# Half-block products in the down projections of a four-FFN network

## The chip, the cores and the metric

The kernel runs on one NeuronCore of one Trainium2 chip. A run's time is the device time in microseconds (us) from the first to the last instruction of the core. All arithmetic is in float32.

## The reference, cut to what matters

The network has 256 tokens, kept as the columns of tiles of 128 features x 256 tokens. Around a series of mixers (MLA attention, an LRU scan, cross attention, sparse attention, a complex state space scan) stand four feed-forward blocks, each of width 2816:

```
def swiglu(h, w_gate_up, w_down):
    g, u = jnp.split(h @ w_gate_up, 2, axis=-1)
    return (jax.nn.silu(g) * u) @ w_down
```

The last two are the same with a short causal convolution on the 5632 up columns. Each is added to the residual stream x, after which comes the next RMS norm. What is changed is `... @ w_down`: a product of a 1024 x 2816 matrix (transposed weights) with 2816 x 256 activations, four times.

## The kernel before, in words

Each engine has its own instruction list, written out by hand and tied to the others by counting semaphores. There is no planner. All weights come as one stream of 128 x 1024 slots (512 KB) through a ring of four SBUF buffers; SyncE issues the load of slot s as soon as slot s-4 is counted in `slot_used`. The loads of a second weight matrix (`ada_in`, 96 loads of 512 KB) stand between those of the stream, and VectorE folds each into a running sum (`ada(n)`, L1679).

A down projection (`down0` to `down3`) makes eight output tiles of 128 features x 256 tokens. Each is 22 matmuls (k tiles 0 to 21 of FFN, three slots of weights), 128x128 weights against 256 columns, all at L395, accumulated in one of four PSUM banks `acc`. The profiler counts two instructions for each float32 matmul. VectorE adds each finished tile to X in `residual` (L1537, with a gain L1539), makes the gained copy that the next stage's first matmuls read (`gain_tile`, L1506) and sums the squares (L1509); ScalarE squares. The next stage begins with `lead`: its first tiles are multiplied from the gained, not yet normalised X (L450), the sum of squares goes through the ones matrix in between (L431, L432), VectorE makes the reciprocal root (L1468, L1458 to L1461) and then normalises H (L1519, L1522) for the following tiles.

Beside the down projections VectorE has other work in its list: in `down0` six `ada` and, after the third tile, `lru_parameters` (small operations on 8 columns, L1802 to L1817); in `down1` `drive_powers`, eight parts of which six have six 512-wide products (L1897 to L1902); ahead of `down2` `local_kernels` (L1924 to L1934), which clears and fills the matrices of the state space stage. In the third up stage TensorE waits for VectorE's `output_powers` (L1918) before the products of L880. The up stages have 44 tiles each, two for every step k of VectorE's loop.

Of the kernel before, what the change touches and what calls it, by code (L numbers as in the profile page):

```python
# [13 lines left out]
P = 128  # L14
# [57 lines left out]
ADA_FREE = [max((b + 1 for b in range(a) if ADA_HOME[b] == ADA_HOME[a]), default=0) for a in range(N_ADA)]  # L72

# [77 lines left out]
def build_program(nc, stream, ada_in, ssm_in, cols_in, x_in, mem_in, pos_in, out):  # L151
    with ExitStack() as ctx:
# [20 lines left out]
        mem_rstd = sb("mem_rstd", S)  # L173
# [6 lines left out]
        keep = sb("keep", S)  # L180
        restart = sb("restart", S)
# [38 lines left out]
        slot_used = sem("slot_used")  # L220
        acc_free = sem("acc_free")
# [106 lines left out]

        block = ctx.enter_context(nc.Block())
# [3 lines left out]
        def _(sp):  # L333
# [37 lines left out]
        def _(pe):  # L371
# [84 lines left out]

            def value_rows(name, src, n):
# [42 lines left out]

            def down(name):

                n = COUNT[name][1]
                for k in range(n):
                    bank_free(TILE0[name] + k)
                    b = acc[(TILE0[name] + k) % 4]
                    for c in range(3):
                        w = slot_in(name, 3 * k + c)
                        lo, hi = 8 * c, min(8 * c + 8, KF)
                        if k == 0:  # L510
                            pe.wait_ge(ffn_mid, 2 + 22 * int(name[-1]) + hi)
                        product(b[:, 0:S], w, [at(FFN, i) for i in range(lo, hi)], first=c == 0, last=c == 2)\
                            .then_inc(slot_used, 1)
# [228 lines left out]
            linear("od_xb", H, lead([("od_xb", 0), ("od_xb", 1)], gained_in_y), first=2)  # L742
# [17 lines left out]
            fresh = lead([("dki", 0)] + [("dqi", k) for k in range(3)], gained_in_late, S + 1, second=M)  # L760
# [243 lines left out]
        def _(act):  # L1004
# [14 lines left out]
            def norm(src, tiles, first=0, after=None, func=ACT.Sqrt):  # L1019
# [6 lines left out]
                if after:  # L1026
                    for k in range(tiles):
                        act.wait_ge(after[0], after[1] + k + 1)
                        nc.scalar.activation(at(SQ, k), at(src, k), ACT.Square).then_inc(norm_squares, 1)  # L1029
# [8 lines left out]
            def double_norm():  # L1038
# [4 lines left out]
                for k in range(KD):  # L1043
                    act.wait_ge(acc_free, 4 + TILE0["down1"] + k + 1)
                    nc.scalar.activation(at(M, k), at(X, k), ACT.Square, scale=col("final_norm", k))
                    nc.scalar.activation(at(SQ, k), at(X, k), ACT.Square).then_inc(norm_squares, 1)
                for e in range(2):
                    act.wait_ge(norm_vars, n + 1 + e)
                    nc.scalar.activation(root[:], variance[:], ACT.Sqrt).then_inc(norm_rstd, 1)
# [202 lines left out]
            norm(X, KD, after=updated("down0"))  # L1252
# [60 lines left out]
            nc.scalar.activation(keep[:], acc[TILE0["dwi"] % 4][:, 0:S], ACT.Copy).then_inc(wi_parts, 1)  # L1313
# [31 lines left out]
            norm(X, KD, after=updated("down2"), func=ACT.Abs_reciprocal_sqrt)  # L1345
# [65 lines left out]
            conv_ffn("up3", 1)  # L1411

# [29 lines left out]
        def _(dve):  # L1442
# [86 lines left out]
            def residual(name, slots_per_tile=1, gain=None, adas_with=0, drive=False, next_gain=None, gained_in=None):  # L1529
                begin(name)  # L1530
                for k in range(8):
                    if drive:
                        drive_powers(k // 4, k % 4)
# [8 lines left out]
                    if name != "down3":  # L1542
                        gain_tile(k, next_gain, gained_in)
                    if name == "down1" and k >= 2:
                        own(v.tensor_tensor(at(M, 0), at(M, 0), at(M, k - 1), ALU.add))
                        if k == KD - 1:
                            dve.sem_inc(norm_summed, 1)
                    if k < adas_with:
                        ada(1)
                    if name == "down0" and k == 2:  # L1550
                        lru_parameters()
# [859 lines left out]
```

## Time and profile before

| | |
|---|---|
| median of 3 runs | 1708.91 us (1708.64 to 1709.92) |
| span of the profiled execution, first to last instruction | 1710.4 us |
| TensorE busy (PE) | 1674.5 us, 98% |
| weight loads (PEld) | 1414.8 us, 83% |
| VectorE busy (DVE) | 775.4 us, 45% |
| ScalarE busy (ACT) | 318.5 us, 19% |
| mean granted TensorE clock | 0.998 |
| moved by DMA | 289.24 MB, mean 169 GB/s |

The page gives no time for the profiled execution other than its span. Busy time is the union of an engine's instructions; neighbouring matmuls overlap, so a mean duration of 379 ns and a busy time of 216 ns for each matmul instruction go together.

### The profile page before, as it was taken

The page shows a single profiled execution, that of the slowest core. Times are in us where ns is not written, and L with a number is a line of the kernel's source. Part 1 is how long each engine was busy: PE and PEld are TensorE (multiplying, and loading weights), DVE is VectorE, ACT ScalarE, POOL GpSimd, SP SyncE. Part 2 cuts the span into 40 slices and gives each one's busy share as a digit, 9 for nine tenths or more (in the row PEclk, how much of TensorE's full clock was granted, in tenths as well). Part 3 has the DMA queues.
Part 4 walks back from the last instruction along what each step waited for, and adds up shares of the span by engine and source line. Part 5 has one row for each costly group of instructions (what it writes and reads, how often), then busy time and mean ns, then how long its engine had stood idle before and what let it go on. Part 6 is the DMA issues. An engine that isn't in the chain of part 4 may idle for free.

```text
span 1710.4 us, 23078 instructions
## 1 busy us (share of the span) xinstructions
PE 1674.5 (98%) x9352; PEld 1414.8 (83%) x9352; DVE 775.4 (45%) x1677; ACT 318.5 (19%) x700; POOL 58.8 (3%) x84
## 2 busy tenths in 40 slices
PE   8999999999999999999999999999999999999998
PEld 6758888888888867888888785788878898788887
DVE  6545354323365414644345576456643183433300
ACT  3241210000042102100000322322211041222200
POOL 0000000000000000191000000000000000000000
PEclk9999999999999999999999999999999999999999
DMA  6445478865654663666554233244434503444455
GB/s 228 138 136 188 144 242 302 293 234 196 210 166 160 225 227 132 249 217 237 184 162 160 87 123 99 87 137 158 148 119 153 169 6 114 138 156 149 157 162 172
DMA packets 79881, 289.24 MB, mean 169 GB/s; under 512 B 8992, under 2 KB 10016, under 8 KB 79264
## 3 DMA queue, kind: packets, MB, share of 16 engines
q1 hardware_dynamic: 79776, 287.76, 50.0%
q8 instruction: 75, 1.23, 0.3%
q14 instruction: 30, 0.25, 0.1%
HBM read 286.68 MB, written 1.05 MB: 168 GB/s over the span
## 4 chain that ended last, share of the span: by engine, by line
PE 94%; DVE 4%; ACT 1%; issue 1%; DMA 0%; SPq 0%; DVEq 0%; ACTq 0%
PE acc L395 72%; PE acc L464 4%; PE acc L960 3%; PE acc L450 3%; PE acc L405 1%; PE score L925 1%; PE acc L939 1%; PE acc L577 1%; PE score L601 1%; PE score L557 1%; PE acc L900 1%; PE acc L628 1%; PE turned L612 0%; PE score L789 0%; PE stat L431 0%
## 5 line engine op out<-in xcount | busy, mean ns | idle before, releaser
L395 PE MATMUL acc<-H,ring 128*128 128x256 f32 x3520 | 772.6, 381 | 6.9 <-DVE H L1522 3.0
L395 PEld LDWEIGHTS acc<-H,ring 128*128 128x128 f32 x3520 | 667.7, 190 | 108.2 <-issue 12.4
L395 PE MATMUL acc<-FFN,ring 128*128 128x256 f32 x1408 | 304.9, 379 | 0.0
L395 PEld LDWEIGHTS acc<-FFN,ring 128*128 128x128 f32 x1408 | 267.3, 190 | 36.8 <-issue 0.4
L395 PE MATMUL acc<-big,ring 128*128 128x256 f32 x880 | 192.1, 379 | 0.9 <-PE acc L395 0.9
L395 PEld LDWEIGHTS acc<-big,ring 128*128 128x128 f32 x880 | 166.9, 190 | 24.6 <-issue 2.0
L1679 DVE SCALAR_TENSOR_TENSOR bT<-bT,cond 128x1024 f32<-128x1024 f32 x58 | 75.7, 1305 | 80.0 <-DMA bT<-ada_in 76.3
L1874 DVE SCALAR_TENSOR_TENSOR pair<-acc,cols,pair 128x255 f32<-128x255 f32 x84 | 40.5, 483 | 132.8 <-ACT pair L1170 129.7
L1537 DVE TENSOR_TENSOR X<-acc,X 128x256 f32<-128x256 f32 x48 | 20.4, 425 | 148.0 <-PE acc L395 138.9
L1170 ACT ACTIVATE pair<-acc,cols 128x256 f32<-128x256 f32 x84 | 47.2, 564 | 173.6 <-PE acc L395 173.6
L1539 DVE SCALAR_TENSOR_TENSOR X<-acc,mod,X 128x256 f32<-128x256 f32 x24 | 11.6, 484 | 144.6 <-PE acc L395 141.2
L1029 ACT ACTIVATE SQ<-X 128x256 f32<-128x256 f32 x56 | 23.4, 417 | 280.2 <-DVE X L1537 187.1
L1150 ACT ACTIVATE pair<-acc 128x256 f32<-128x256 f32 x42 | 16.1, 383 | 261.3 <-PE acc L395 261.3
L450 PE MATMUL acc<-FFN,ring 128*128 128x256 f32 (+1 forms) x224 | 52.7, 389 | 7.2 <-DMA ring<-stream 7.2
L464 PE MATMUL acc<-ring,big 128*128 128x512 f32 x128 | 56.2, 593 | 1.6 <-DVE big L1989 1.6
L1837 DVE TENSOR_TENSOR FFN<-pair,acc 128x256 f32<-128x256 f32 x42 | 17.7, 421 | 87.9 <-PE acc L395 83.7
L960 PE MATMUL acc<-MEM,ring 128*128 128x256 f32 x256 | 56.3, 381 | 0.1
L450 PEld LDWEIGHTS acc<-FFN,ring 128*128 128x128 f32 x224 | 43.7, 196 | 13.7 <-issue 7.2
L960 PEld LDWEIGHTS acc<-MEM,ring 128*128 128x128 f32 x256 | 48.3, 190 | 7.2 <-ACT MEM L1389 0.5
L1679 DVE SCALAR_TENSOR_TENSOR bT<-big,cond,bT 128x1024 f32<-128x1024 f32 x26 | 33.4, 1285 | 34.9 <-DMA big<-ada_in 34.0
L464 PEld LDWEIGHTS acc<-ring,big 128*128 128x128 f32 x128 | 24.2, 190 | 29.6 <-issue 27.3
L1424 POOL TENSOR_SCALAR chunk_tab<-cols,small 128x64 f32<-128x64 f32 x32 | 18.3, 614 | 718.0 <-DVEq L1736 718.0
(421 smaller groups left out, 1356.0 us busy)
## 6 DMA issues: line engine op xcount, KB each, us to landing
ring<-stream SPq DMA_DIRECT2D x440, 512.0 KB, 3.5
bT<-ada_in SPq DMA_DIRECT2D x70, 512.0 KB, 4.4
big<-ada_in SPq DMA_DIRECT2D x26, 512.0 KB, 4.5
big<-ssm_in SPq DMA_DIRECT2D x2, 1024.0 KB, 5.7
cols<-cols_in SPq DMA_DIRECT2D x1, 1165.5 KB, 8.5
X<-x_in SPq DMA_DIRECT2D x4, 256.0 KB, 4.6
MEM<-mem_in SPq DMA_DIRECT2D x1, 1024.0 KB, 11.8
y_out<-X SPq DMA_DIRECT2D x8, 128.0 KB, 3.4
```

The source lines that it names most:

```text
L395: mm = nc.tensor.matmul(dst, w[:, k * cols_per:(k + 1) * cols_per], r, start=first and n == 0, stop=last and n == len(src) - 1)
L405: mm = nc.tensor.matmul(acc[TILE0[name] % 4][:, 0:S], w[:, k * P:(k + 1) * P], at(src, k), start=k == 0, stop=k == KD - 1)
L450: mm = nc.tensor.matmul(acc[t % 4][:, 0:width], w[:, k * P:(k + 1) * P], src(k, width), start=k == 0, stop=k == KD - 1)
L464: mm = nc.tensor.matmul(acc[(t + b) % 4][:, :], src[:, k * S + b * P:k * S + b * P + P], w[:, k % 2 * 512:(k % 2 + 1) * 512], start=k == 0 ...
L960: mm = nc.tensor.matmul(acc[(TILE0["glu"] + k) % 4][:, 0:S], w[:, i * P:(i + 1) * P], at(MEM, i), start=n == 0, stop=n == KD - 1)
L1029: nc.scalar.activation(at(SQ, k), at(src, k), ACT.Square).then_inc(norm_squares, 1)
L1170: nc.scalar.activation(at(pair, 2 * (k % 2) + e), at(FFN, 10 + e) if k == 0 else acc[(TILE0[name] + 2 * k + e) % 4][:, 0:S], ACT.Identity, ...
L1424: ins = g.tensor_scalar(r[:, st * CHUNKS:(st + 1) * CHUNKS], time, turns_hi[:, st:st + 1], None, ALU.mult)
L1537: v.tensor_tensor(at(X, k), b, at(X, k), ALU.add).then_inc(acc_free, 1)
L1679: own(v.scalar_tensor_tensor(sums, row, cond[:, k:k + 1], sums, ALU.mult, ALU.add))
L1837: v.tensor_tensor(at(FFN, k), at(pair, k % 2), up, ALU.mult).then_inc(acc_free, 2)
L1874: own(v.scalar_tensor_tensor(pair[:, z + 1:z + S], b[:, 0:S - 1], col("fconv_w", c + (3 * layer + 1) * 44), pair[:, z + 1:z + S], ALU.mult ...
```

## The change

The 1024 x 2816 weights of a down projection are cut into four pairs of output tiles, and each pair into three chunks of 8, 8 and 6 k tiles. In a chunk the weights are a 2 x 2 grid of blocks (two output tiles, two halves of the k tiles) and the activations a 2 x 2 grid (two halves of the k tiles, two halves of 128 tokens). Winograd's form of Strassen's scheme takes seven block products in place of eight. Three use weights or activations as they are (two both, one with summed activations), four use sums of weights that VectorE makes (`sum_weights`: 4 operations of 512 or 384 columns a chunk, 12 chunks a projection) in one set of four buffers. Sums of activations (`sum_mids`: 4 operations) are made three times a projection. Every matmul now has 128 columns. Results of a pair are put together by ScalarE (`corner`) and VectorE (`combine_upper`, `combine`). A ring slot is released when TensorE has used it and VectorE has summed it.

Other edits: six of eight `drive_powers` move from `down1` to steps 16 to 21 of the second up stage, and what stood there moves to earlier steps; `late_lead` takes the place of `lead` after `down0` and `down1` (k rows 0 to 5 of two tiles, then the rest, and the sum of squares after the first tile in place of after its fourth k row); the root after them is ScalarE's reciprocal root, and VectorE's reciprocal is left out; buffers share room.

```diff
@@ sync
                 sp.wait_ge(slot_used, s + 1)
+                if s - RING in FAST_SLOT:
+                    sp.wait_ge(weight_sums, 4 * FAST_SLOT[s - RING] + 4)
@@ tensor
+            def late_lead(tiles, src, width=S, last=KD - 1, whole=False, second=None):
...
+                for js, rows in ((range(2), range(6)), (range(2), range(6, KD)), (range(2, len(tiles)), range(KD))):
...
+            def block_product(dst, w, x, first=False, last=False):
+
+                for k in range(len(x)):
+                    mm = nc.tensor.matmul(dst, w[:, k * P:(k + 1) * P], x[k], start=first and k == 0,
+                                          stop=last and k == len(x) - 1)
+                return mm
+
             def down(name):
...
+                for j in range(4):
+                    t = TILE0[name] + 2 * j
+                    bank_free(t + 1)
+                    a, b = acc[t % 4], acc[(t + 1) % 4]
                     for c in range(3):
...
+                        block_product(a[:, 0:P], w[:, 0:h * P], x[0][0], first=first)
+                        block_product(a[:, 2 * P:3 * P], w[:, h * P:2 * h * P], x[1][0])
+                        if j == 0:
+                            pe.wait_ge(mid_sums, 3 * i + c + 1)
+                        if c < 2:
+                            block_product(b[:, P:2 * P], w2[:, h * P:2 * h * P], d4, first=first).then_inc(slot_used, 2)
+                        for e in sum_order(c):
+                            if c == 2 and e == 0:
+                                block_product(b[:, P:2 * P], w2[:, h * P:2 * h * P], d4, first=first).then_inc(slot_used, 2)
...
+                            pe.wait_ge(weight_sums, 4 * n + e + 1)
+                            block_product(dst, summed_weights[e], d, last=last and e in (1, 3)).then_inc(weight_sums_used, 1)
@@ vector
+            def sum_order(c):
+                return (2, 3, 0, 1) if c == 2 else (0, 1, 2, 3)
...
+            def sum_weights(name, n):
...
+                for e, (dst, x, y, op) in enumerate(((s3, a11, a21, ALU.subtract), (s1, a21, a22, ALU.add),
+                                                     (s2, s1, a11, ALU.subtract), (s4, a12, s2, ALU.subtract))):
+                    if n:
+                        dve.wait_ge(weight_sums_used, sum_uses(name, n - 1, e))
+                    v.tensor_tensor(dst, x, y, op).then_inc(weight_sums, 1)
+                    dve.wait_ge(weight_sums, 4 * d + e + 1)
...
+            def paired_residual(name, gain=None, adas_with=0, drive=False, next_gain=None, gained_in=None):
+                begin(name)
+                for j in range(4):
+                    for c in range(3):
+                        if 3 * j + c + 1 < 12:
+                            sum_weights(name, 3 * j + c + 1)
+                        if c and 2 * j + c - 1 < adas_with:
+                            ada(1)
+                    if drive:
+                        if j < 2:
+                            drive_powers(1, 2 + j, H)
+                    if name == "down0" and j == 1:
                         lru_parameters()
...
+                    dve.wait_ge(corner_out, 4 * int(name[-1]) + j + 1)
+                    combine_upper(a, home)
+                    dve.wait_ge(weight_sums_used, 4 * (CHUNK0[name] + 3 * j + 3))
+                    outs_of = combine(a, b, home, score[0])
+                    for k, b in zip((2 * j, 2 * j + 1), outs_of):
...
@@ the second up stage
-                    if layer == 1 and 14 <= k < 20:
-                        input_product(k - 14)
+                    if layer == 1 and 10 <= k < 16:
+                        input_product(k - 10)
+                    if layer == 1 and k >= 16:
+                        drive_powers((k - 16) // 4, (k - 16) % 4, late)
@@ end of the convolution's up stages
+                    if k in (8, 16):
+                        sum_mids(layer + 2, k // 8 - 1)
+                sum_weights(f"down{layer + 2}", 0)
+                sum_mids(layer + 2, 2)
                 if s5:
                     local_kernels()
-                residual(f"down{layer + 2}", 3, lambda k: mod_col(layer, 5, k))
+                paired_residual(f"down{layer + 2}", lambda k: mod_col(layer, 5, k))
@@ vector, after down0
-            inverse_rms(rstd[:])
+            inverse_rms(rstd[:], first=root[:])
```

## Rows read from the trace of the kernel before

**Rows 1.** The page: busy time (us, share, instructions); the chain that ended last.

```profile
PE 1674.5 (98%) x9352; PEld 1414.8 (83%) x9352; DVE 775.4 (45%) x1677; ACT 318.5 (19%) x700; POOL 58.8 (3%) x84
...
PE 94%; DVE 4%; ACT 1%; issue 1%; DMA 0%; SPq 0%; DVEq 0%; ACTq 0%
```

**Rows 2.** The page, groups: line, operation, count, busy us, mean ns, idle before.

```profile
L395 PE MATMUL acc<-FFN,ring 128*128 128x256 f32 x1408 | 304.9, 379 | 0.0
```

**Rows 3.** Window of down0: stretch, each engine's busy us and count, granted clock, DMA.

```profile
386.70:462.70 76.00, 76.00 (x356) 66.91 (x353) 22.23 (x72) 2.92 (x7) 0.00 (x0) 1.00 0.61 207
```

**Rows 4.** Timeline of PE: start us, length us, line, operation, shapes, count.

```profile
115.21 0.83 PE L612 MATMUL stat<-pair,probs 128*128 128x128 f32 x6
115.88 0.83 PE L612 MATMUL turned<-pair,probs 128*128 128x128 f32 x6
...
1373.11 2.00 PE L925 MATMUL score<-FFN,bT 128*128 128x64 f32 x16
```

**Rows 5.** Groups of DVE by shape: count, busy us, mean ns, idle before.

```profile
L1679 DVE SCALAR_TENSOR_TENSOR bT<-bT,cond 128x1024 f32<-128x1024 f32 x58 | 75.7, 1305 | 80.0 <-DMA bT<-ada_in 76.3 <-DVE FFN L1837 0.8 <-DVE bT L1679 0.5
...
L1539 DVE SCALAR_TENSOR_TENSOR X<-acc,mod,X 128x256 f32<-128x256 f32 x24 | 11.6, 484 | 144.6 <-PE acc L395 141.2 <-PE acc L405 3.2 <-DVE late L1934 0.2
...
L1506 DVE TENSOR_SCALAR FFN<-X,modgain 128x256 f32<-128x256 f32 x16 | 5.7, 354 | 0.6
```

**Rows 6.** Timeline of DVE at the start of down1, two of six operations.

```profile
849.89 0.69 DVE L1897 TENSOR_TENSOR H<-MEM,powers 128x512 f32<-128x512 f32 x1
850.62 0.69 DVE L1898 TENSOR_TENSOR H<-MEM,powers 128x512 f32<-128x512 f32 x1
```

**Rows 7.** Timeline of DVE in down0: first and last row of 46, and the next.

```profile
418.08 0.17 DVE L1802 TENSOR_SCALAR small<-cols 128x8 f32<-128x8 f32 x1
...
427.28 0.17 DVE L1817 TENSOR_SCALAR softp<-small 128x8 f32<-128x8 f32 x1
427.60 0.42 DVE L1537 TENSOR_TENSOR X<-acc,X 128x256 f32<-128x256 f32 x1
```

**Rows 8.** Timeline of DVE at the start of down2.

```profile
1291.20 0.42 DVE L1882 TENSOR_TENSOR FFN<-pair 128x256 f32<-128x256 f32 x1 [0.54 <-ACT pair L1175]
1292.23 1.76 DVE L1924 MEMSET big<- 128x2048 f32 x1 [0.60 <-DVE FFN L1882]
...
1303.77 1.51 DVE L1934 SCALAR_TENSOR_TENSOR late<-cols,late 128x128 f32<-128x128 f32 x4
```

**Rows 9.** Timeline of PE in the third up stage; then the window after the stall.

```profile
1256.28 0.45 PE L880 MATMUL score<-big,MEM 128*32 128x32 f32 x16 [3.15 <-DVEq L1919]
...
1256.50:1262.20 5.70, 5.70 (x44) 4.44 (x37) 0.78 (x2) 0.00 (x0) 0.00 (x0) 0.50 0.00 0
```

**Rows 10.** Timelines of PE and DVE after down0.

```profile
465.45 5.34 PE L450 MATMUL acc<-big,ring 128*128 128x256 f32 x24
470.71 0.45 PE L395 MATMUL acc<-H,ring 128*128 128x256 f32 x1
...
465.73 0.42 DVE L1468 TENSOR_SCALAR variance<-stat 128x256 f32<-128x256 f32 x1 [0.57 <-PE stat L432]
466.64 1.75 DVE L1458 RECIPROCAL rstd<-root 128x256 f32<-128x256 f32 x1 [0.48 <-ACT root L1036]
```

**Rows 11.** Timelines of PE and DVE after down1.

```profile
928.58 12.34 PE L450 MATMUL acc<-late,ring 128*128 128x257 f32 x56
942.18 0.67 PE L395 MATMUL acc<-H,ring 128*128 128x256 f32 x2 [1.26 <-issue]
...
939.36 0.35 DVE L1522 TENSOR_SCALAR H<-H,mod 128x256 f32<-128x256 f32 x1
941.02 0.16 DVE L1646 COPY shifts<-acc 128x1 f32<-128x1 f32 x1 [1.30 <-PE acc L450]
```

**Rows 12.** Timeline of PE after down2; then the page's DMA issues of `ada_in`.

```profile
1366.99 0.67 PE L431 MATMUL stat<-SQ,ones 128*128 128x256 f32 x2 [1.21 <-DVEq L1513]
...
bT<-ada_in SPq DMA_DIRECT2D x70, 512.0 KB, 4.4
```

More of the change, by code:

```diff
@@ L72 @@
 ADA_FREE = [max((b + 1 for b in range(a) if ADA_HOME[b] == ADA_HOME[a]), default=0) for a in range(N_ADA)]
+FAST = [(f"down{i}", 4, 3) for i in range(4)]
+PAIR0, CHUNK0, FAST_SLOT = {}, {}, {}
+_pairs = _chunks = 0
+for _name, _m, _c in FAST:
+    PAIR0[_name], CHUNK0[_name] = _pairs, _chunks
+    for _j in range(_m * _c):
+        FAST_SLOT[SLOT0[_name] + 2 * _j] = FAST_SLOT[SLOT0[_name] + 2 * _j + 1] = _chunks + _j
+    _pairs, _chunks = _pairs + _m, _chunks + _m * _c
+HALF = P
+DOWN_TILES = (4, 4, 3)
 PARTS0, _n = {}, 0
@@ L455, in lead @@
                 return before
+            def late_lead(tiles, src, width=S, last=KD - 1, whole=False, second=None):
+                before = outs[0]
+                outs[0] += 4
+                for js, rows in ((range(2), range(6)), (range(2), range(6, KD)), (range(2, len(tiles)), range(KD))):
+                    for j in js:
+                        name, tile = tiles[j]
+                        w = slot_in(name, tile)
+                        t = TILE0[name] + tile
+                        bank_free(t)
+                        for k in rows:
+                            if j == 0:
+                                leads[0] += 1
+                                pe.wait_ge(gained, leads[0])
+                            mm = nc.tensor.matmul(acc[t % 4][:, 0:width], w[:, k * P:(k + 1) * P], src(k, width),
+                                                  start=k == 0, stop=k == KD - 1)
+                        if rows[-1] == KD - 1:
+                            mm.then_inc(slot_used, 1)
+                            if j == 0:
+                                sums(last, whole, second)
+                return before
             def value_rows(name, src, n):
@@ L759, in _ @@
             ada_cols_of(1)
-            fresh = lead([("dki", 0)] + [("dqi", k) for k in range(3)], gained_in_late, S + 1, second=M)
+            fresh = late_lead([("dki", 0)] + [("dqi", k) for k in range(3)], gained_in_late, S + 1, second=M)
             def project(name, k, fresh=None):
@@ L1250, in _ @@
             swiglu("up0", 0)
-            norm(X, KD, after=updated("down0"))
+            norm(X, KD, after=updated("down0"), func=ACT.Abs_reciprocal_sqrt, paired="down0")
             begin("od_xb")
@@ L1541, in residual @@
                     dve.wait_ge(acc_free, 4 + TILE0[name] + k + 1)
[L1542 to L1547, printed above, removed]
+                    gain_tile(k, next_gain, gained_in)
                     if k < adas_with:
@@ new lines, in sum_mids @@
+            def sum_mids(i, c):
+                if i == 1 and c == 1:
+                    dve.wait_ge(s5_angle, 1)
+                (b11, b12), (b21, b22) = mid_blocks(c)
+                t2, t3, t4 = (home[:, 0:P * DOWN_TILES[c]].rearrange("p (k t) -> p k t", t=HALF)
+                              for home in mid_sum_homes(i, c))
+                own(v.tensor_tensor(t3, b22, b12, ALU.subtract))
+                own(v.tensor_tensor(b12, b12, b11, ALU.subtract))
+                own(v.tensor_tensor(t2, b22, b12, ALU.subtract))
+                own(v.tensor_tensor(t4, b21, t2, ALU.subtract))
+                dve.sem_inc(mid_sums, 1)
@@ L1839, in swiglu @@
                     dve.sem_inc(ffn_mid, 1)
+                    if k in (8, 16):
+                        sum_mids(layer, k // 8 - 1)
+                sum_weights(f"down{layer}", 0)
+                sum_mids(layer, 2)
                 ada_rows_of(layer)
```

149 lines of the change are left out of this document (109 added, 40 removed).

## The prediction

> **What bounds the kernel now.** I read the page first: TensorE is busy 98% of the span and carries 94% of the chain that ended last, VectorE 4% [rows 1]. So time is won only in TensorE's list, and work of VectorE costs only where TensorE comes to wait for it. The group of the down projections has 1408 instructions in 304.9 us, 216.5 ns each and 76.2 us for a projection [rows 2]; the window of down0 shows no idle time and full clock [rows 3]. So the products themselves are what there is to save, and the first question is what an instruction of 128 columns takes.
>
> **The products.** Before: 4 x 8 x 22 matmuls of two instructions, 1408. After: a pair has 7 x (4 + 4 + 3) = 77 block matmuls, a projection 4 x 77 x 2 = 616 instructions, four of them 2464. Two runs of six with 128 columns start 0.67 us apart, 111.7 ns each, across a wait that was already met [rows 4]. Sixteen with only 64 columns take 2.00 us, so (2.00 - 0.28 for the last one's length) / 15 = 115 ns [rows 4]: halving the columns again gains nothing, so here the 128x128 weight load sets the pace and not the columns. I take 111.7 ns: a projection of 68.8 us, 7.4 us less, **29.4 us saved** over four. The low end is half of 216.5, 108.3 ns (8 us less in all); the high end is 115 ns (8 us more, the gain down to 21).
>
> The Trainium skill (TensorE: Matmul & The Clock Gate, "Back-to-back issue gap") gives some 81 ns a matmul sustained for 128 columns in a stream of load and matmul pairs. By it 2464 instructions take 200 us in place of 275. Its section "LDWEIGHTS" gives columns / 1.2, 107 ns, for a load that this stream can't hide, and the trace's 111.7 stands near that and not near 81.
>
> **VectorE's pace inside a projection.** A block of four k tiles is 8 instructions, 0.89 us, of three 0.67; a chunk 6.26 us, the third 4.69, a pair 17.2. Operations of 512 columns follow each other at 0.73 us [rows 6], 256 at 0.42 + 0.04 = 0.46 [rows 8], with a gain 0.52 and a scaling 0.36 [rows 5], and for 384 I take 0.59 between the two; 128 columns 0.38 (four in 1.51) [rows 8]. The sum buffers are single: each of a chunk's sums waits until TensorE has used the same one of the chunk before. After the last block of a pair, VectorE still has three sums of the next chunk (2.2 us, 2.3 with the signal), then `combine` (0.46 x 3 + 0.38 = 1.8), the residual part, and then the first sum of the chunk after (0.73 + 0.1). TensorE has meanwhile one chunk and three direct blocks: 6.26 + 2.68 = 8.94 us of cover. Without extras VectorE needs 4.9 us and the residual part: 2 x (0.46 + 0.36 + 0.46) = 2.6 in down0, 3.5 in down1 (one addition more), 2.0 in down2 and down3. All are below 8.94. What stands in between decides:
>
> - down0, second pair: one `ada` (1.31) [rows 5] and `lru_parameters`, 418.08 to 427.60, 9.5 us [rows 7]. 4.9 + 2.6 + 1.3 + 9.5 = 18.3, so TensorE stands **9.3 us**.
> - down0, third pair: the sixth `ada_in` load is issued when chunk 8's slots are released, its fifth block, and lands 4.4 us later [rows 12]; VectorE waits for it: **1.0 us** late.
> - down1, first pair: the part of `drive_powers` that stays, 6 x 0.73 = 4.4. 4.9 + 1.7 + 4.4 = 11.0: **2.0 us**. Second pair: two copies, 1.3: 4.9 + 3.5 + 1.3 = 9.7: **0.8 us**. Third pair: 8.4, hidden.
> - down2: VectorE's last product of the up stage ends 2.1 us after TensorE's start; then come sum_weights 2.9, sum_mids 2.4, and `local_kernels`, 1292.23 to 1305.28, 13.0 [rows 8], and the first sum of chunk 1: ready at 21.2. TensorE needs it at 0.25 + 8.93 = 9.2: **12.0 us**. The first sum of chunk 0 costs 0.25 in down2 and down3 each.
>
> Together 25.6 us. Before, TensorE needed nothing of these two: it waited only for free banks, which residuals give back.
>
> **The clock.** After 3.15 us of idle TensorE ran the window 1256.5 to 1262.2 at granted clock 0.50, that is 1.2 GHz [rows 9]. In those 5.2 us or so of slow matmuls half the work is done. I take 2.5 us after each of the stalls of 9.3 and 12.0 (between 0 and 5), and none after those of 2 us.
>
> **Into the next stage.** down0: 24 lead instructions (rows 0 to 5) take 5.2 us and cover the late pair (last gained tile 3.4 us after the end). But the sum of squares now stands after tile 0, and only 0.9 us of work behind it. The chain from there took 470.71 - 465.45 = 5.26 us and loses the reciprocal and its gap, 1.8 [rows 10]: 3.5 against 0.9, **2.6 us** of wait where there was none. down1: behind the sums stand 0.9 + 6.9 = 7.8 us; normalising H ended 939.71 - 928.58 = 11.1 after them, less 1.8 is 9.3, and the first bank comes free 1.2 later: 10.5 against 7.8 is 2.7, where it was 1.26 [rows 11]. Net **1.2** with the order of the lead. down2: three operations of `combine` and tile 6 (0.52 + 0.46) come ahead of tile 7: **2.2 us** later to the sums, on top of 1.21 us of idle [rows 12]. 3.4 us of idle is nearest to the 3.15 that cost the clock, so another **2.5** (0 to 2.5). down3: the same without the squares, **1.8**.
>
> **What is hidden.** Moved `drive_powers`: 6 x 0.73 + 1.31 + 0.46 = 6.2 us in a step of 32 x 0.2165 = 6.9; sum_mids at step 16 (2.9) makes VectorE 2 us late at most and TensorE has two banks, a whole step, of cover. A step or more of slack also takes sum_mids in the other up stages; the stall before L880 stays. Loads: a chunk's 1 MB has 10 us from release to use, against 3 to 5 us from issue to landing.
>
> **Sum.** 25.6 (stalls) + 5.0 + 2.5 (clock) + 2.6 + 1.2 + 2.2 + 1.8 (seams) = 40.9; less 29.2 (76.1 - 68.8, four times, by the window) is **+11.7 us**: a span of 1722.1 for the 1710.4 of the profile. The median of the runs is 1.5 us below that span, so I predict **1720.6 us**.
>
> **Rivals.**
> 1. The detours don't bite. If `lru_parameters` and `local_kernels` ran in the shade of more than 8.94 us, 9.3 + 12.0 + 5.0 go and the time is 1694.3, faster. It decides at a detour of some 1.5 us in down0 and 1 us in down2. For it: VectorE is 45% busy. Against: its list is in order and the buffers single. 8%.
> 2. Bubbles at blocks. Four of seven blocks begin with a wait for weights just written. If the first load of such a block can't be made ahead, it costs one load's pace, 0.11 us [rows 4]. 192 such places x 0.11 = 21 us: 1742. Against: the second run of rows 4 starts without a gap. 9%.
> 3. No change. No half clock (-7.5) and 108.3 ns (-8), with local stalls a little shorter: 1705 to 1712. 7%.
> 4. Loads hide and narrow instructions overlap more than wide ones, so that they come at three quarters of half of 216.5 ns, 81: 2464 x 30.5 ns = 75 us less, 1645. Against it all of rows 4. 1%. (It is the pace of the Trainium skill's section above.)
> The forecast itself has 75%, its own range 1713 to 1728.
>
> **Chances.** This measurement can't tell less than 0.2%, 3.4 us, from no change. Faster: rivals 1 and 4, 0.09. Within: rival 3, 0.07. Slower: the forecast and rival 2, 0.84. The range of 8 in 10 leaves out rivals 1 and 4 and the far part of 2: 1710 to 1731.
>
> **What would show it.** Matmul instructions in the projections: 2464 at 111 to 112 ns outside of stalls. One TensorE stall of 9 us some 43 us into down0 and one of 12 us some 9 us into down2, each released by a sum of weights, each followed by granted clock 0.5. Stalls of 2 and 0.8 in down1, 2.6 after down0. down3 should be near 69 us. I am wrong if VectorE's sums stand well ahead of TensorE at those places, if the pace is under 105 or over 116 ns, or if the clock stays full.

## The result, and the profile after

The changed kernel takes **1728.22 us** (median of 4, 1727.5 to 1730.98); the kernel before, run beside it, 1709.41 (1708.64 to 1712.35). The ratio is 1.0108, with a 95% interval of 1.0094 to 1.0122: slower by 1.1%. Forecast were 1720.6 us and a range of 1710 to 1731. Of all runs below one stands apart, 2930.15 us at a mean granted clock of 0.556 in e5, and is left out of that experiment's figures.

The page after: busy time with its share and instructions, the chain that ended last, and two groups.

```profile
PE 1653.2 (96%) x10408; PEld 1429.3 (83%) x10408; DVE 952.4 (55%) x1978; ACT 323.9 (19%) x717; POOL 62.8 (4%) x84
...
PE 88%; DVE 8%; issue 1%; ACT 1%; DMA 1%; SPq 0%; DVEq 0%; ACTq 0%
...
L572 PE MATMUL acc<-FFN,ring 128*128 128x128 f32 x760 | 93.8, 276 | 0.0
...
L1662 DVE TENSOR_TENSOR probs_t<-ring 128x512 f32<-128x512 f32 (+1 forms) x96 | 62.1, 647 | 64.5 <-PE acc L572 56.7
```

Against [rows 1] TensorE has 21.3 us less busy time, VectorE 177 us more, and VectorE's share of the chain has gone from 4% to 8%. L572 is the half-block product; L1662 makes the sums of weights that it waits for. The mean of 276 ns isn't its pace: lengths in these rows overlap, as in [rows 4], and I take paces from start to start.

The windows of the four projections, in the columns of [rows 3]:

```profile
385.90:467.90 82.00, 71.86 (x620) 71.39 (x617) 57.61 (x132) 3.61 (x10) 0.00 (x0) 0.94 0.52 183
859.20:931.00 71.80, 69.47 (x620) 69.08 (x617) 49.65 (x94) 5.91 (x16) 0.00 (x0) 1.00 0.47 164
1297.00:1381.40 84.40, 72.03 (x616) 71.62 (x616) 56.24 (x96) 9.65 (x15) 0.00 (x0) 0.92 0.42 144
1649.00:1719.00 70.00, 69.11 (x618) 68.88 (x616) 42.70 (x74) 2.09 (x6) 0.00 (x0) 1.00 0.51 174
```

The first column of busy time is TensorE's: 69 to 72 us in every one, but down0 and down2 last 82 and 84. Idle time makes most of that, and a granted clock of 0.94 and 0.92 the rest. The stalls themselves, in the timeline of PE (the bracket is the idle time before, and its releaser):

```profile
438.81 2.08 PE L572 MATMUL acc<-big,probs_t 128*128 128x128 f32 x8 [9.17 <-DVE probs_t L1662]
...
446.18 0.83 PE L572 MATMUL acc<-H,pair 128*128 128x128 f32 x6
446.85 0.83 PE L572 MATMUL acc<-FFN,pair 128*128 128x128 f32 x6
...
478.44 0.89 PE L441 MATMUL acc<-H,ring 128*128 128x256 f32 x3 [2.44 <-DVE H L1622]
...
766.46 5.85 PE L441 MATMUL acc<-H,ring 128*128 128x256 f32 x26 [3.56 <-DVE FFN L2015]
...
887.35 1.16 PE L572 MATMUL acc<-chunk_tab,probs_t 128*128 128x128 f32 x8 [1.78 <-DVE probs_t L1662]
905.45 1.16 PE L572 MATMUL acc<-chunk_tab,probs_t 128*128 128x128 f32 x8 [0.55 <-DVE probs_t L1662]
...
949.35 1.19 PE L441 MATMUL acc<-H,ring 128*128 128x256 f32 x2 [2.43 <-issue]
...
1318.76 2.07 PE L572 MATMUL acc<-rope,probs_t 128*128 128x128 f32 x8 [12.26 <-DVE probs_t L1662]
...
1384.99 0.67 PE L477 MATMUL stat<-SQ,ones 128*128 128x256 f32 x2 [3.43 <-DVEq L1616]
...
1652.81 1.16 PE L572 MATMUL acc<-probs,probs_t 128*128 128x128 f32 x8 [0.89 <-DVE probs_t L1662]
```

Two runs of six that wait for nothing start 446.85 - 446.18 = 0.67 us apart, as before the change. A stall costs a little more than its bracket. The bracket begins at the end of the last matmul, 0.28 us after its start, and the next one would have started 0.11 us after it: taken from start to start, the first stall is 9.34 us. And the windows behind three of the stalls:

```profile
438.80:443.80 5.00, 4.99 (x23) 5.00 (x24) 3.17 (x5) 0.00 (x0) 0.00 (x0) 0.50 0.35 101
...
1318.80:1324.00 5.20, 5.20 (x24) 5.20 (x25) 3.13 (x5) 0.00 (x0) 0.00 (x0) 0.50 0.38 117
...
1386.00:1389.00 3.00, 3.00 (x9) 2.37 (x8) 2.19 (x6) 1.56 (x4) 0.00 (x0) 0.50 0.01 3
```

TensorE was granted half its full clock, 1.2 of 2.4 GHz: 23 narrow instructions took 5 us where at full clock they take 2.6.

The whole account, from the starts of matmuls in the two traces (span 1710.4 before, 1725.8 after):

| stretch | before | after | change | forecast |
|---|---|---|---|---|
| up to down0 | 386.67 | 385.88 | -0.8 | 0 |
| down0 | 75.86 | 81.96 | +6.1 | +5.6 |
| from down0 to down1 | 386.2 | 391.3 | +5.1 | +2.6 |
| down1 | 75.86 | 71.73 | -4.1 | -4.4 |
| from down1 to down2 | 364.95 | 366.0 | +1.1 | +1.2 |
| down2 | 75.86 | 84.36 | +8.5 | +7.5 |
| from down2 to down3 | 263.6 | 267.8 | +4.2 | +4.7 |
| down3 | 75.86 | 69.83 | -6.0 | -7.0 |
| after down3 | 5.6 | 6.9 | +1.3 | +1.8 |
| sum | 1710.4 | 1725.8 | +15.4 | +12 |

(A projection is counted from its first to its last start, what lies between two from there to the next first start; this moves the forecast's sum of 11.7 by a few tenths.)

### The profile page after: what moved, and what is told of

The parts are those of the page before. It is cut to its first block, busy times and chain, and to the rows that moved or that the text cites. A ratio compares the mean times of both kernels' runs of the same rounds, so it can differ in the third digit from the quotient of the medians.

```text
span 1725.8 us, 25861 instructions
## 1 busy us (share of the span) xinstructions
PE 1653.2 (96%) x10408; PEld 1429.3 (83%) x10408; DVE 952.4 (55%) x1978; ACT 323.9 (19%) x717; POOL 62.8 (4%) x84
## 4 chain that ended last, share of the span: by engine, by line
PE 88%; DVE 8%; issue 1%; ACT 1%; DMA 1%; SPq 0%; DVEq 0%; ACTq 0%
PE acc L441 54%; PE acc L572 13%; PE acc L532 4%; PE acc L1050 3%; PE acc L496 2%; PE acc L517 1%; PE acc L451 1%; PE score L1015 1%; PE acc L1029 1%; PE acc L667 1%; PE score L691 1%; PE score L647 1%; DVE probs_t L1662 1%; PE acc L990 1%; PE acc L718 1%
## 5 line engine op out<-in xcount | busy, mean ns | idle before, releaser
L1662 DVE TENSOR_TENSOR probs_t<-ring 128x512 f32<-128x512 f32 (+1 forms) x96 | 62.1, 647 | 64.5 <-PE acc L572 56.7
L572 PE MATMUL acc<-FFN,ring 128*128 128x128 f32 x760 | 93.8, 276 | 0.0
L572 PEld LDWEIGHTS acc<-FFN,ring 128*128 128x128 f32 x760 | 89.1, 192 | 0.7 <-issue 0.4
L496 PEld LDWEIGHTS acc<-FFN,ring 128*128 128x128 f32 x224 | 43.4, 194 | 13.7 <-issue 7.4
L572 PE MATMUL acc<-FFN,probs_t 128*128 128x128 f32 x352 | 48.9, 282 | 0.0
L572 PE MATMUL acc<-FFN,pair 128*128 128x128 f32 x352 | 47.3, 276 | 0.0
```

The costliest lines, as they stand in the source:

```text
L496: mm = nc.tensor.matmul(acc[t % 4][:, 0:width], w[:, k * P:(k + 1) * P], src(k, width), start=k == 0, stop=k == KD - 1)
L572: mm = nc.tensor.matmul(dst, w[:, k * P:(k + 1) * P], x[k], start=first and k == 0, stop=last and k == len(x) - 1)
L1662: v.tensor_tensor(dst, x, y, op).then_inc(weight_sums, 1)
```

## The experiments

Each group had runs of the kernel before on its own chip: median 1710.8 beside e1 to e4, 1710.46 beside e5 to e8, 1709.91 beside e9 to e12. Ratios are against those. The change itself took 1729.84 us in the third group (e12) and 1728.22 above, so a difference of 1 or 2 us between medians of different groups shows nothing by itself.

**e1, the recurrence's parameters taken out of down0.**

```diff
-                    if name == "down0" and j == 1:
-                        lru_parameters()
@@ first up stage, behind ada()
+                    if layer == 0 and k == 18:
+                        lru_parameters()
```

> The changed kernel with lru_parameters taken out of VectorE's list between the second and third pair of down0 and put at step 18 of the first up stage. Theory (VectorE's list is in order and its four sum buffers are single, so a detour beyond 8.94 us of cover is a stall of TensorE): the stall of 9.3 us in down0 and its half clock (2.7 us) go, and none comes in the up stage, where two banks cover a step: 12 us less than 1728.2, so about 1716. Rival (the stall is of weights that land late, or of TensorE's own bubbles, and not of the detour): a wait of some 9 us stays at the same chunk, time within 2 us of 1728.

Measured: 1723.76 us, ratio 1.0075 [1.0059, 1.0091]. The stall of 9.3 us is gone and down0 takes 70.67 us, 11.3 less (9.3 and most of the half clock behind it). That shows the cause of this stall. But the median fell by only 4.5 us where I expected 12. VectorE's and TensorE's timelines in the first up stage:

```profile
362.70 1.28 DVE L1853 SCALAR_TENSOR_TENSOR bT<-bT,cond 128x1024 f32<-128x1024 f32 x1 [5.15 <-DMA bT<-ada_in]
```
```profile
374.35 4.14 PE L441 MATMUL acc<-H,ring 128*128 128x256 f32 x11 [3.50 <-DVE FFN L2015]
```

At the new place the 9.5 us stood behind an `ada` that had itself waited 5.15 us for its load. Together they were more than the cover of the up stage's banks, TensorE stood 3.67 us and lost some 1.5 to the clock. I had counted the instructions that were moved and not the wait ahead of them. The profiled execution also has 1.2 GHz behind the waits after down0 (474.3 to 477.6) and in the second up stage (764.4 to 767.8), where the change's profile has full clock. But it has full clock behind the wait of 3.15 us in the third up stage (PE's timeline, then the window):

```profile
1264.05 0.33 PE L970 MATMUL score<-big,MEM 128*32 128x32 f32 x16 [3.15 <-DVEq L2108]
```
```profile
1262.00:1270.00 8.00, 5.96 (x85) 4.87 (x86) 3.83 (x6) 0.57 (x1) 0.00 (x0) 1.00 0.24 77
```

The kernel before had half clock behind the same wait [rows 9].

**e2, the local kernels cut into five parts** between the sums and the pairs of down2.

```diff
-                if s5:
-                    local_kernels()
@@ paired_residual
+                        if name == "down2" and c < 2 and 2 * j + c < 5:
+                            local_kernels(2 * j + c)
```

> The changed kernel with local_kernels cut into five parts, each behind one of the first sums of weights of down2 (parts of 4.0, 2.9, 2.9, 1.5, 1.5 us), its combined products in another PSUM bank. Theory: the stall of 12.4 us early in down2 and its half clock (2.7 us) go, and no part is long enough to stall: 15 us less, about 1713. Rival (VectorE has no room left in a projection, sums 8.2 and results 3.8 of 17.2 us a pair with waits in between): the 13 us come back as stalls of 2 to 4 us at several chunks, at most 5 us less, 1723 or more.

Measured: 1716.67 us (8 runs), ratio 1.0035 [1.0023, 1.0048]: 11.6 us less than the change. down2 takes 73.67 us in place of 84.36. The median came 3 to 4 us over the expected 1713. One new stall is left, at the sums behind the first and largest part, with granted clock 0.50 after it (1317.2 to 1320.6):

```profile
1317.29 1.62 PE L572 MATMUL acc<-H,pair 128*128 128x128 f32 x6 [2.71 <-DVE pair L1662]
```

**e3, the moved steps of the scan each set one step later** (decays at step 8, where they were before the change, factors at 9).

```diff
-                    if layer == 1 and k in (2, 7, 8):
+                    if layer == 1 and k in (2, 8, 9):
-                        (... state_decays if k == 7 else ...)
+                        (... state_decays if k == 8 else ...)
```

> The changed kernel with state_decays back at step 8 of the second up stage and input_factors at step 9 (they were at 7 and 8). Theory: at step 7 four VectorE operations of 0.2 us lasted 1.13 us each while GpSimd ran its 512-wide additions; one step later GpSimd is past them. The stall of 3.7 us in that stage falls to the 1.0 us it had before: 2.7 us less, about 1725.5. Rival (the stall is of the amount of work put in steps 7 and 8, or of the sum_mids put at step 8): it stays at 3 us or more and moves one step.

A miss: 1733.64 us, ratio 1.0132 [1.0117, 1.0147], slower than the change. There are now two stalls, the second larger than the one it was to remove:

```profile
770.48 7.14 PE L441 MATMUL acc<-H,ring 128*128 128x256 f32 x32 [0.88 <-DVE FFN L2015]
...
782.13 2.47 PE L441 MATMUL acc<-H,ring 128*128 128x256 f32 x5 [4.51 <-DVE FFN L2015]
```

The first stall did fall back to what it was before the change (0.86 us there), as the theory said. The second is new: at step 9 `input_factors` now come behind the sum_mids of step 8 (3.1 us) and an `ada`, and run into GpSimd's next four operations of 512 columns (L1538). VectorE's timeline, two of three slow operations, then GpSimd's:

```profile
777.45 1.22 DVE L1946 TENSOR_TENSOR small<-small 128x32 f32<-128x32 f32 x1
...
778.93 1.14 DVE L1948 TENSOR_TENSOR small<-small,cols 128x32 f32<-128x32 f32 x1
```
```profile
777.36 5.40 POOL L1538 TENSOR_TENSOR chunk_tab<-chunk_tab 128x512 f32<-128x512 f32 x4
```

In the change the same operations of `input_factors` took 0.25 us. The three together cost 2.7 us more here, and half clock (0.50 from 781.4 to 788.0) follows the stall. So the move out of one collision led into the next; e10 takes the collision away.

**e4, the kernel before with each product of 256 columns as two of 128.** No Strassen, no sums.

```diff
-                        product(b[:, 0:S], w, [at(FFN, i) for i in range(lo, hi)], first=c == 0, last=c == 2)\
+                        for q in range(2):
+                            mm = product(b[:, q * P:q * P + P], w,
+                                         [FFN[:, i * S + q * P:i * S + q * P + P] for i in range(lo, hi)],
+                                         first=c == 0 and q == 0, last=c == 2 and q == 1)
```

> The kernel before with each matmul of 256 columns in the down projections cut into two of 128, same weights loaded twice, no sums and no other change: TensorE's pace at 128 columns alone. 2816 instructions in place of 1408. If the weight load sets the pace (111.7 ns): 314.6 us for 304.4, so 10 us more than before, 1719. If the columns do (108.3 ns): no change, 1709. If narrow instructions overlap to 81 ns: 76 us less, 1633.

Measured: 1722.31 us, ratio 1.0069 [1.0052, 1.0086]. The window of down0:

```profile
386.50:465.20 78.70, 78.70 (x708) 78.70 (x705) 22.25 (x72) 2.92 (x7) 0.00 (x0) 1.00 0.62 200
```

704 instructions in 78.6 us are 111.7 ns each, with TensorE and its weight loads both busy all the time; with 256 columns the loads were busy 66.91 of 76.00 us [rows 3]. Halving the columns doesn't quite halve an instruction (108.3 ns would be half of 216.5). Each keeps its own load of 128x128 weights, and by these rows that load sets the pace. Seven of eight such products, 616, are 68.8 us: 9.6% less than 76.1, not 12.5%.

**e5, the clock by itself.** Throwaway matmuls on TensorE in the two long waits: 20 in down0, 27 in down2.

```diff
+                            if (name, 3 * j + c, e) in (("down0", 7, 0), ("down2", 1, 0)):
+                                for _ in range(20 if name == "down0" else 27):
+                                    nc.tensor.matmul(turned[0][:, 0:S], ident, col("tri", 0, S), start=True, stop=True)
                             pe.wait_ge(weight_sums, 4 * n + e + 1)
```

> The changed kernel with matmuls of no use (identity by a constant, 20 and 27 of 256 columns, into a free bank) in TensorE's list just ahead of the two long waits of down0 and down2, so that TensorE is busy while it would stand. The waits for VectorE stay. Theory: after both the granted clock stays at 1.00, and the 23 and more instructions at half pace (0.10 us each) go: 2.7 us each, 5.4 us less, about 1723. Rival (the slow stretch is not of the clock but of loads that restart after a wait, or the added matmuls run over the stall's end): no gain or a loss, 1728 or more.

The waits stay and are filled (first two lines, PE's timeline), and the window behind them has full clock (third):

```profile
430.51 8.80 PE L604 MATMUL turned<-cols 128*128 128x256 f32 x40
440.00 1.16 PE L572 MATMUL acc<-big,probs_t 128*128 128x128 f32 x8 [0.69 <-DVE probs_t L1665]
```
```profile
438.00:444.00 6.00, 5.31 (x42) 4.79 (x41) 5.64 (x12) 0.42 (x1) 0.00 (x0) 1.00 0.15 25
```

down0 takes 79.81 us and down2 81.97, 2.15 and 2.4 less than in the change: the price of the half clock, where the forecast had 2.5. The runs took 1726.17, 1726.69 and 1727.63 us (ratio 1.0096 [1.0081, 1.0112]), so the median moved by only 1.5 us where I expected 5.4. The profiled execution had half clock elsewhere, behind the waits after down0 and in the second up stage, where the change's profile has full clock; e12 comes back to this.

**e6, the sums of squares after the sixth tile in place of the first,** so that the seam after a projection has more to do.

```diff
-                            if j == 0:
-                                sums(last, whole, second)
@@ late_lead
+                    if rows[-1] == 5:
+                        sums(last, whole, second)
```

> The changed kernel with the sum of squares after down0 and down1 put behind the first 24 lead instructions (k rows 0 to 5) in place of behind tile 0. Theory (the chain from the sums to the normalised H takes 3.5 us, and only 0.9 us of matmuls cover it after down0): 0.87 us more cover there, the wait of 2.6 us falls to 1.7; after down1 from 2.6 to 1.7: 1.7 us less in all, about 1726.5. Rival (the squares of tile 7 aren't ready at that place): TensorE waits for the sums in their place and gains nothing.

Measured: 1725.14 us, ratio 1.0086 [1.0072, 1.01]. The waits after down0 and down1 go from 2.60 and 2.59 to 1.74 and 1.72, for example:

```profile
476.80 1.53 PE L441 MATMUL acc<-H,ring 128*128 128x256 f32 x6 [1.57 <-DVE H L1622]
```

**e7, the scan powers put back into down1,** all of them, for the part of the change that moved them.

```diff
-                    if layer == 1 and k >= 16:
-                        drive_powers((k - 16) // 4, (k - 16) % 4, late)
@@ paired_residual, down1
-                        if j < 2:
-                            drive_powers(1, 2 + j, H)
+                        drive_powers(j // 2, 2 * (j % 2), H)
+                        drive_powers(j // 2, 2 * (j % 2) + 1, H)
```

> The changed kernel with all eight drive_powers back in down1, two behind the sums of each pair, as many us as they had before: the projection change without the move. Theory: the detour is 8.7 us in the first and third pair, 5.7 in the second and fourth; by need less 8.94 of cover TensorE stands about 6.3, 5.1 and 8.1 us in down1 in place of 2.0, 0.8 and 0, two or three of them with half clock after: 17 to 24 us more, 1745 to 1752. Rival (the move bought little, since VectorE had room in down1 as well): within 3 us of 1728.

Measured: 1754.22 us, ratio 1.0258 [1.0242, 1.0274]; down1 takes 93.16 us.

```profile
895.26 2.08 PE L572 MATMUL acc<-chunk_tab,probs_t 128*128 128x128 f32 x8 [6.25 <-DVE probs_t L1662]
...
918.75 1.65 PE L572 MATMUL acc<-chunk_tab,probs_t 128*128 128x128 f32 x6 [4.66 <-DVE probs_t L1662]
...
945.86 2.07 PE L572 MATMUL acc<-chunk_tab,probs_t 128*128 128x128 f32 x8 [8.09 <-DVE probs_t L1662]
```

From start to start the stalls are 6.4, 4.8 and 8.2 us, within 0.3 us of what the rule of cover (8.94 us against the sum of VectorE's work in between) gave. Moving this work was worth 26 us: without that move the seven products would have lost 2.6%.

**e8, the edits of e1, e2, e3 and e6 together.**

> The changed kernel with four edits together: lru_parameters in the first up stage, local_kernels in five parts, state_decays at step 8, the sums of squares earlier after down0 and down1. Theory: the gains add, 12 + 15 + 2.7 + 1.7 = 31 us less than 1728.2: about 1697, 0.7% below the kernel before. Rival (one stall taken away shows the next one behind it): 1705 to 1712, no better than before.

Measured: 1711.35 us (11 runs), ratio 1.001 [0.9999, 1.0021]: no better than the kernel before, some 14 us over what I expected and in the rival's band. The stalls that e1, e2 and e3 had each left came along: 3.71 us in the first up stage, 4.64 in the second, 2.87 in down2. In the profiled execution, one of the two fastest of the 11 (1707.25 us), half clock follows the first two and not the third.

**e9, each of those leftovers mended.** The parameters go ahead of `ada` at step 18, so that VectorE's wait for the load comes after them; the local kernels come in six parts from the second chunk on, their two fills apart; `state_decays` go to step 8, the scan's factors to step 10, its products to 11 to 15 and sum_mids to 12; the sums of e6; and seven throwaway matmuls after down2 keep the clock.

```diff
+                    if layer == 0 and k == 18:
+                        lru_parameters()
                     ada(2 if layer == 0 and k < 14 else 1)
-                    if layer == 1 and k in (2, 7, 8):
+                    if layer == 1 and k in (2, 8, 10):
-                    if layer == 1 and 10 <= k < 16:
-                        input_product(k - 10)
+                    if layer == 1 and 11 <= k < 16:
+                        input_product(k - 11)
+                    if layer == 1 and k == 15:
+                        input_product(5)
-                    if k in (8, 16):
-                        sum_mids(layer, k // 8 - 1)
+                    if k in (12 if layer else 8, 16):
+                        sum_mids(layer, k // 8 - 1 if k != 12 else 0)
+                        if name == "down2" and c < 2 and 1 <= 2 * j + c < 7:
+                            local_kernels(2 * j + c - 1)
             down("down2")
+            for _ in range(7):
+                nc.tensor.matmul(score[1][:, 0:S], ident, col("tri", 0, S), start=True, stop=True)
```

> The changed kernel with the detours placed by what the runs before showed: lru_parameters at step 18 of the first up stage but ahead of the ada that waits for its load (behind it, it came 5 us late and stalled TensorE 3.7 us); local_kernels in six parts from the second chunk of down2 on, none longer than 2.9 us; state_decays at step 8, input_factors at 10, sum_mids of the second up stage at 12; the sums of squares earlier after down0 and down1; 7 matmuls of no use behind down2 to keep the clock. Theory: of the four-edit kernel's 1711, the stalls of 3.7, 2.9 and 4.6 us and some 5 us of half clock go: about 1696, 0.8% below the kernel before. Rival (gains of this kind don't add, a next stall stands behind each): 1703 to 1710.

Measured: **1693.62 us** (1693.16 to 1694.19), ratio 0.99 [0.9886, 0.9915], the first version faster than the kernel before, by 1%. The windows of its projections:

```profile
385.80:455.90 70.10, 69.41 (x620) 69.01 (x617) 49.79 (x86) 3.61 (x10) 0.00 (x0) 1.00 0.61 212
843.60:915.50 71.90, 69.57 (x622) 69.06 (x617) 49.73 (x94) 5.91 (x16) 0.00 (x0) 1.00 0.48 164
1280.40:1349.60 69.20, 69.10 (x620) 68.91 (x617) 56.26 (x96) 9.70 (x15) 0.00 (x0) 1.00 0.50 176
1616.00:1685.90 69.90, 69.01 (x617) 68.80 (x615) 42.70 (x74) 2.09 (x6) 0.00 (x0) 1.00 0.52 174
```

Full clock in all four, and 281.0 us from first to last start for the four together, 22.4 less than before and 27 less than in the change. The kernel before has no such extra matmuls; what of the 1% they bring by themselves was not separated. They can hold back only the half clock after down2, which cost the change some 1.5 us in that stage, so by this estimate they bring at most a tenth of the 16 us.

**e10, the second up stage's stall.** GpSimd's four subtractions of `state_decays` are left out, so the scan's tables hold other values; VectorE's work is as in the change.

```diff
-            for q in quarters:
-                own(g.tensor_tensor(r[:, q], r[:, q], whole[:, q], ALU.subtract))
```

> The changed kernel without GpSimd's four 512-wide subtractions, so its chunk_tab isn't what it should be. A test of what made state_decays long at step 7 of the second up stage. If the collision with these subtractions did it: no VectorE operation there of 1.13 us any more, state_decays 3.7 us shorter, and the stall of 3.7 us in that stage at 0 to 1. If it was the place in VectorE's list alone: stall within 0.3 us of 3.7.

In the change, VectorE's timeline and GpSimd's over the same stretch:

```profile
752.91 0.19 DVE L2409 TENSOR_TENSOR small<-small 128x32 f32<-128x32 f32 x1
753.13 1.13 DVE L2410 TENSOR_SCALAR small<-small 128x32 f32<-128x32 f32 x1
754.30 0.19 DVE L2409 TENSOR_TENSOR small<-small 128x32 f32<-128x32 f32 x1
754.52 1.13 DVE L2410 TENSOR_SCALAR small<-small 128x32 f32<-128x32 f32 x1
```
```profile
752.91 5.50 POOL L1533 TENSOR_TENSOR chunk_tab<-chunk_tab 128x512 f32<-128x512 f32 x4
```

and in e10 VectorE and, at the place of the stall, TensorE:

```profile
755.16 0.19 DVE L2407 TENSOR_TENSOR small<-small 128x32 f32<-128x32 f32 x1
755.38 0.24 DVE L2408 TENSOR_SCALAR small<-small 128x32 f32<-128x32 f32 x1
```
```profile
757.65 13.60 PE L441 MATMUL acc<-H,ring 128*128 128x256 f32 x61
```

Without those subtractions, adding a constant to 32 columns (L2410, in e10 L2408) takes 0.24 us in place of 1.13, four times 0.9 us less, and TensorE's stall of 3.7 is gone. Its one run took 1728.26 us, though, and its span 1726.5. The profile has half clock behind the wait after down0 (478.8 to 482.2) and a longer stretch of it in the third up stage than the change's has, so this run shows the cause of the stall and no gain.

The slow operations start 754.52 - 753.13 = 1.39 us apart, the pace of GpSimd's four (5.50 / 4 = 1.38): by these starts each ends only when one of GpSimd's ends. The Trainium skill (SBUF — State Buffer, "SBUF: two separate sides") says that VectorE and GpSimd share a pair of ports as an exclusive lock, held for a whole instruction, and that it is taken on VectorE's side by operations in a 2-port mode, or with two inputs in SBUF against a GpSimd operation that reads SBUF. The trace agrees on the lock; whether L2410 ran in such a mode no row shows. The products of two tensors between them (L2409) take 0.19 us in this place, each starting as GpSimd goes from one instruction to the next; e3's slow operations are of that kind (TENSOR_TENSOR) and take 1.14 to 1.22.

**e11, the old lead in place of `late_lead`.**

```diff
-late_lead([
+lead([
```

> The changed kernel with lead in place of late_lead after down0 and down1: the sum of squares again behind the fourth k row of tile 0. Theory: the last pair's results come 3.4 to 4.8 us after TensorE's end, so TensorE now waits for the sum of squares itself, some 2.2 us after down0 and 3 us after down1; behind it 5.2 us of matmuls cover the chain of 3.5 us, so the wait of 2.6 us there goes. Both seams come out within 1 us of what they are: 1727 to 1730. Rival (late_lead is what costs the seams): 2 us or more less.

A miss, on the far side: 1733.56 us, ratio 1.0135 [1.0119, 1.0152]. PE's timeline at the two seams has these waits:

```profile
472.82 0.67 PE L477 MATMUL stat<-SQ,ones 128*128 128x256 f32 x2 [1.99 <-DVEq L1616]
...
939.52 0.67 PE L477 MATMUL stat<-SQ,ones 128*128 128x256 f32 x2 [2.90 <-DVEq L1729]
...
956.61 1.75 PE L441 MATMUL acc<-H,ring 128*128 128x256 f32 x7 [1.26 <-issue]
```

After down0 the wait only changes its place (2.2 for 2.6); after down1 there are two, 3.1 and 1.4, for one of 2.6. So the new order of the lead is worth about 1.9 us after down1 and little after down0. Beside e12, the change on the same chip, the median is 3.7 us longer. Part of the rest is the clock: the window 940.0 to 944.0, behind the wait of 2.9 us, has granted clock 0.57, where e12 has full clock after down1. What remains stays open.

**e12, the changed kernel once more,** to see what differs from execution to execution.

> The changed kernel itself, once more, beside the three above on one chip. It should be 1727 to 1731; its profile shows whether half clock follows the waits of 2.6 and 3.7 us (after down0, after down1, in the second up stage) or not, which the profile of the first run had only in part. If the runs of one kernel differ by such stretches, each of 1.5 us, that is why its runs spread over 3.5 us.

Measured: 1729.84 us, ratio 1.0108 [1.0093, 1.0123], with the same stalls to 0.2 us. What differs is the clock behind the shorter ones. The window after the stall in the second up stage, in the first profile of the change and then in this one:

```profile
766.40:771.00 4.60, 4.54 (x21) 4.05 (x22) 4.04 (x12) 0.38 (x1) 4.60 (x8) 1.00 0.47 134
```
```profile
766.00:771.00 5.00, 4.64 (x14) 3.82 (x15) 4.32 (x14) 0.00 (x0) 5.00 (x10) 0.66 0.43 125
```

After 3.6 us of idle time the clock stayed full once and fell once. After down1 it was the other way about: half clock behind the wait in the first profile, none here. In the third up stage both have it behind the wait of 3.15 us, for 3.4 us in the first profile and 6.8 here, and e1, e5 and e8 have none there. Each such fall costs about 1.5 us or twice that, so that two falls more or less would make the 3.5 us between the change's fastest and slowest run.

## Why the prediction was right, and where it was off

- **The pace, 111.7 ns: right.** A projection without extras takes 68.8 us; e9's down2 has 69.18 and e4 gives the same pace without any of the change. Rival 4 (81 ns) is refuted, and rival 2 as well: 192 waits at 0.11 us would have made down3 some 5 us longer, and it takes 69.83 with 1.06 us of stall in it. Rivals 1 and 3 fall with the stalls of 9.34 and 12.43 us and the half clock behind them.
- **Cover of 8.94 us against VectorE's detours: right.** Forecast and measured: down0 9.3 and 9.34, then 1.0 and 1.13; down1 2.0 and 1.95, 0.8 and 0.71; down2 12.0 and 12.43, 0.25 and 0.27. e1 and e2 removed the two causes and the stalls went; e7 added to a third and it grew as computed. Only down3 was under-counted: 1.06 for 0.25, the first sum of chunk 0, at 1652.81. VectorE makes it behind its last product of the up stage:

```profile
1651.41 0.43 DVE L2064 TENSOR_TENSOR FFN<-pair 128x256 f32<-128x256 f32 x1 [0.54 <-ACT pair L1276]
```

That product ends 2.8 us after TensorE's first matmul of down3 (1649.07). The forecast took the 2.1 us of down2 for both; ahead of down2, and not of down3, TensorE has 0.6 us of kernel products (L970, L973) behind the last up product.
- **The clock: right in down0 and down2** (2.5 each; e5 shows 2.15 and 2.4). In the state space stage after down2 1.5 us came for 2.5. What the forecast left out is that stalls of 2.6 to 3.7 us may cost it too, in some executions, and that the half clock of [rows 9] is itself there in some executions only.
- **Seams: right.** After down0 2.60 for 2.6, after down1 2.59 for 2.7, after down2 3.59 - 1.37 = 2.2 for 2.2, the tail 1.3 for 1.8.
- **The step that failed: "What is hidden".** It priced the steps moved in the second up stage at nothing, by counting the 6.2 us of `drive_powers` and sum_mids and their cover. `state_decays`, one step earlier than before, was not looked at beside GpSimd: the stall there grew from 1.02 to 3.72 us, +2.7, because four operations of VectorE took 0.9 us more each while GpSimd worked (e10).
- **"The median of the runs is 1.5 us below that span": true of the kernel before, wrong to carry over.** The time of a run of these kernels is its span plus 1.7 to 1.9 us (e7: 2.0). Runs of before with a span of 1710.4 took 1712.2 us, so the profiled execution was most likely its slowest, 1712.35. Of the 33 runs of before beside the experiments, the 12 with a mean granted clock of 0.998 took 1711.06 to 1713.12 us, the 21 with 0.999 or 1.000 took 1708.43 to 1711.18. The profile has 0.998, and its half clock of [rows 9] lasts 6.8 us (by estimate some 3 us of time). So the shorter executions most likely have less of it; only this one was profiled. Of the 18.8 us between the medians, 15.4 are seen in the two traces, and the rest is this.

Together: the forecast was 7.6 us low. Of that 3.7 are in the span (2.7 for the missed stall, about 1 each for down2 and down3, less what the state space stage and the tail cost less, and less 0.8 up to down0, where e12's profile of the same kernel has 386.4 us for 385.9 and executions differ by as much); 3.25 come from the step from span to run (plus 1.75 in place of less 1.5), and 0.7 from the median lying above the profiled run.

So the gain of the products was there: 303.4 us from first to last start in the four projections before, 307.9 after, of which 26.9 are stalls and 4.6 half clock, leaves 276.4, 27 us less (forecast 29.2). It was given back by detours that an in-order list puts between two sums (the 26.9 us), by the half clock behind them, and by seams that had less to do.

## What to carry to other kernels

- When one engine begins to feed another through single buffers, work out the consumer's cover for one period (here 8.94 us) and set beside it everything that stands in the producer's in-order list in between, each wait for a load included. Here that sum gave each stall in the projections to within 0.5 us, but one, and showed what to cut up or move: down2 alone gained 11 us from local kernels in five parts.
- Seven products for eight save an eighth of the work only if the pace per column stays; here narrow float32 products fell to the pace of their weight loads (111.7 ns for 128 columns, 216.5 for 256) and the saving was 9.6%.
- When small operations are moved, look at what GpSimd runs at the new place and at what wait stands ahead of it; both cost a stall here that a count of durations does not show.

## What the runs showed of the hardware

- Idle time of TensorE and the clock behind it are not a fixed pair: 9 and 12 us were followed by 1.2 GHz each time. The same wait of 3.15 us was in the kernel before [rows 9], in the change and in e12, and not in e1, e5 and e8; 2.6 and 3.6 us (after down1, in the second up stage) in some executions of the same kernel only. Which one it will be isn't in any row that I found.
- An operation of 128x32 on VectorE takes 0.19 to 0.25 us alone and 1.13 to 1.22 us when it starts behind a GpSimd operation of 128x512 (1.38 us each); TENSOR_SCALAR did in the change, TENSOR_TENSOR in e3.
